# Up-projection of an MLP in fp32r with weight pieces stationary and 256 tokens moving, and the norm factor moved to the residual add

## The reference

```python
def rmsnorm(x, w):
    y = xf * lax.rsqrt(jnp.mean(xf * xf, axis=-1, keepdims=True) + EPS)
    return (y * w.astype(jnp.float32)).astype(x.dtype)

def sqrelu_mlp(h, w_up, w_down):        # w_up 2048 x 8192, w_down 8192 x 2048
    u = jax.nn.relu(h @ w_up)
    return (u * u) @ w_down

for layer in range(2):
    ...
    x = x + y.astype(x.dtype)           # y of the mixer or the attention
    h = rmsnorm(x, norm_mlp_w[layer])
    x = x + sqrelu_mlp(h, mlp_w_up[layer], mlp_w_down[layer]).astype(x.dtype)
return rmsnorm(x, final_norm_w)
```

## Time and profile before

| | |
|---|---|
| median of 3 runs | 2051.8 us (2050.81 to 2052.05) |
| span of the profiled execution, its own time | 2050.5 us |
| TensorE (PE) matmul busy | 2007.7 us, 98% |
| TensorE weight load (PEld) busy | 1655.0 us, 81% |
| DVE busy | 1422.5 us, 69% |
| ACT busy | 1019.8 us, 50% |
| DMA | 382.49 MB, mean 187 GB/s |

### The profile page before, as it was taken

How to read it: one execution, slowest core, us unless ns; L and a number is a source line. 1 busy time by engine, 2 the same in 40 slices (tenths; PEclk the granted TensorE clock), 3 DMA queues, 4 the chain that set the end, 5 groups by cost and what they waited for, 6 DMA issues and landing times.

```text
span 2050.5 us, 24784 instructions
## 1 busy us (share of the span) xinstructions
PE 2007.7 (98%) x9195; PEld 1655.0 (81%) x9195; DVE 1422.5 (69%) x1931; ACT 1019.8 (50%) x1343; POOL 43.3 (2%) x55
## 2 busy tenths in 40 slices
PE   8999999999999999999999999999999999999997
PEld 6888888877888788788887877878888888788886
DVE  5776678887467657756888677878548656855864
ACT  5566665454345435434555554555345434534543
POOL 1110110000000000000000000000000000000000
PEclk9999999999999999999999999999999999999999
DMA  8555546655656556556655544566566566556552
GB/s 291 171 171 204 184 156 211 189 175 196 199 178 205 189 190 192 189 192 191 198 174 197 165 140 149 186 193 196 185 192 197 185 191 196 183 192 196 185 192 100
DMA packets 191612, 382.49 MB, mean 187 GB/s; under 512 B 6184, under 2 KB 6448, under 8 KB 191408
## 3 DMA queue, kind: packets, MB, share of 16 engines
q1 hardware_dynamic: 190288, 377.58, 56.8%
q0 software_dynamic: 1216, 3.88, 0.6%
q10 hardware_dynamic: 32, 0.01, 0.0%
HBM read 379.34 MB, written 2.10 MB: 186 GB/s over the span
## 4 chain that ended last, share of the span: by engine, by line
PE 83%; DVE 9%; ACT 4%; issue 3%; DMA 0%; ACTq 0%; SPq 0%; DVEq 0%
PE acc L1018 27%; PE acc L1020 27%; PE acc L1019 27%; DVE turn L887 3%; DVE w_lo L701 3%; ACT w_hi L516 2%; PE bank L1029 1%; ACT stage L561 0%; PE bank L1108 0%; DVE b_lo L709 0%; DVE a_lo L713 0%; ACT L580 0%; PE bank L1118 0%; PE bank L1132 0%; ACT area L606 0%
## 5 line engine op out<-in xcount | busy, mean ns | idle before, releaser
L701 DVE TENSOR_TENSOR w_lo<-raw,w_hi 128x1024 fp32r<-128x1024 f32 x712 | 867.0, 1225 | 560.6 <-ACT w_hi L516 558.1
L516 ACT ACTIVATE w_hi<-raw 128x1024 fp32r<-128x1024 f32 x712 | 748.5, 1059 | 845.3 <-PE acc L1020 845.2
L1018 PE MATMUL acc<-w_hi,a_hi 128*128 128x512 f32 x1568 | 617.1, 394 | 5.0 <-DVE a_lo L713 4.7
L1020 PE MATMUL acc<-w_hi,a_lo 128*128 128x512 f32 x1568 | 611.9, 390 | 0.0
L1019 PE MATMUL acc<-w_lo,a_hi 128*128 128x512 f32 x1568 | 611.7, 390 | 0.0
L1018 PE MATMUL acc<-w_hi,b_hi 128*128 128x512 f32 x1280 | 500.2, 391 | 13.1 <-DVE b_lo L709 10.9
L1020 PE MATMUL acc<-w_hi,b_lo 128*128 128x512 f32 x1280 | 498.7, 390 | 0.0
L1019 PE MATMUL acc<-w_lo,b_hi 128*128 128x512 f32 x1280 | 498.7, 390 | 0.0
L1018 PEld LDWEIGHTS acc<-w_hi,a_hi 128*128 128x128 f32 x1568 | 295.0, 188 | 69.0 <-DVE a_lo L713 6.0
L1020 PEld LDWEIGHTS acc<-w_hi,a_lo 128*128 128x128 f32 x1568 | 294.8, 188 | 61.6
L1019 PEld LDWEIGHTS acc<-w_lo,a_hi 128*128 128x128 f32 x1568 | 295.0, 188 | 60.0
(11 more groups left out here) (152 smaller groups left out, 522.4 us busy)
## 6 DMA issues: line engine op xcount, KB each, us to landing
raw<-in_mlp_w_up SPq DMA_DIRECT2D x128, 1024.0 KB, 5.6
raw<-in_mlp_w_down SPq DMA_DIRECT2D x128, 1024.0 KB, 5.1
raw<-in_hyb_w_in SPq DMA_DIRECT2D x48, 1024.0 KB, 5.2
raw<-in_attn_w_qkv SPq DMA_DIRECT2D x20, 1024.0 KB, 5.1
raw<-in_hyb_w_out SPq DMA_DIRECT2D x16, 1024.0 KB, 5.2
raw<-in_attn_w_out SPq DMA_DIRECT2D x16, 1024.0 KB, 5.1
x<-in_x SPq DMA_DIRECT2D x4, 512.0 KB, 9.8
out_y<-x SPq DMA_DIRECT2D x4, 512.0 KB, 4.0
```

The source lines that it names most:

```text
L516: nc.scalar.activation(w_hi[:, h % RING], raw[:, h // 2, 2 * (h % 2):2 * (h % 2) + 2, :], ACT.Copy).then_inc(hi_ready, 1)
L701: nc.vector.tensor_tensor(w_lo[:, h % RING], raw[:, h // 2, 2 * (h % 2):2 * (h % 2) + 2, :], w_hi[:, h % RING].bitcast(F32), ALU.subtract) ...
L1018: nc.tensor.matmul(a, xh, wh, start=first, stop=False)
L1020: ins = nc.tensor.matmul(a, xl, wh, start=False, stop=last)
```

## The change

In an up block the operands change places: the stationary one is now a 128x128 piece of the weights, the moving one the 256 tokens of a row tile of `a_hi` or `a_lo`. The result comes out with hidden columns on the partitions and tokens along them, as the down blocks need it; the two halves of a bank hold two pieces of 128 hidden columns. The turn by DVE is gone for up blocks. A factor per token can't be applied per partition any more; since relu(s h) squared is s squared times relu(h) squared for positive s, the norm factor is squared (`rinv2`) and multiplied in where the down block's result is added to `x`.

```diff
-BY_QUADRANT = {"up", "res"}
+BY_QUADRANT = {"res"}
+AS_TURNED = {"up"}
...
+            def leave_up(slot):
+
+                b = slot.b - 1
+                act.wait_ge(turned_out, slot.count(N_TURNED, -1, INIT_HALVES))
+                for m in range(2):
+                    nc.scalar.activation(stage[:, m, :], acc[:, b % 2, m, :], ACT.Relu).then_inc(evac_act, 1)
+                for m in range(2):
+                    act.wait_ge(evac_act, slot.count(N_EVAC_ACT, -1, m + 1))
+                    nc.scalar.activation(stage[:, m, :], stage[:, m, :], ACT.Square).then_inc(squared, 1)
+
+            def up_hi(slot, j):
+
+                for m in range(2):
+                    act.wait_ge(squared, slot.count(N_SQUARED, -1, m + 1))
+                    nc.scalar.activation(b_hi[:, COLS * j + 2 * m:COLS * j + 2 * m + 2, :],
+                                         stage[:, m, :].rearrange("p (k s) -> p k s", k=2),
+                                         ACT.Copy).then_inc(turned_hi, 1)
...
+                if kind == "up" and k == 1:
+                    up_hi(slot, j)
...
+                ins = nc.vector.reciprocal(rinv[:, norm, :], rms[:, norm, :])
+                if norm in (1, 3):
+                    link(ins)
+                    ins = nc.vector.tensor_tensor(rinv2[:, norm, :], rinv[:, norm, :], rinv[:, norm, :], ALU.mult)
+                ins.then_inc(rinv_ready, 1)
...
+            def up_lo(slot, j):
+
+                for m in range(2):
+                    dve.wait_ge(turned_hi, slot.count(N_SPLIT, -1, INIT_HALVES + m + 1))
+                    to = slice(COLS * j + 2 * m, COLS * j + 2 * m + 2)
+                    nc.vector.tensor_tensor(b_lo[:, to, :], stage[:, m, :].rearrange("p (k s) -> p k s", k=2),
+                                            b_hi[:, to, :].bitcast(F32), ALU.subtract).then_inc(turned_out, 1)
...
+                        if norm is None:
+                            ins = nc.vector.tensor_tensor(xs, xs, y, ALU.add)
+                        else:
+                            ins = nc.vector.scalar_tensor_tensor(xs, y, rinv2[:, norm, tt:tt + 1], xs,
+                                                                 ALU.mult, ALU.add)
...
+                if kind == "up" and k == 2:
+                    up_lo(slot, j)
...
+                if BLOCKS[b][0] == "up":
+                    up_products(b, k).then_inc(half_used, 1)
+                    return
...
+            def up_products(b, k):
+
+                for e in range(2):
+                    kt = 2 * k + e
+                    xh, xl = a_hi[:, kt, :], a_lo[:, kt, :]
+                    for f in range(COLS):
+                        wh, wl = (w[:, k % RING, e, f * P:(f + 1) * P] for w in (w_hi, w_lo))
+                        a = acc[:, b % 2, f // 2, (f % 2) * SEQ:(f % 2 + 1) * SEQ]
+
+                        first, last = k == 0 and e == 0 and f % 2 == 0, k == HALVES - 1 and e == 1
+                        nc.tensor.matmul(a, wh, xh, start=first, stop=False, skip_group_check=True)
+                        nc.tensor.matmul(a, wh, xl, start=False, stop=False, skip_group_check=True)
+                        ins = nc.tensor.matmul(a, wl, xh, start=False, stop=last, skip_group_check=True)
+                return ins
```

More of the change, by code:

```diff
@@ L90 @@
 TURNED = {"xb", "gate", "q", "k", "g", "kv", "aq", "up", "res"}
-BY_QUADRANT = {"up", "res"}
+BY_QUADRANT = {"res"}
+AS_TURNED = {"up"}
 SPLIT = {"g", "up", "res"}
 PLAIN = TURNED - SPLIT
+THROUGH_TURN = TURNED - AS_TURNED
 FROM_STAGE = {"xb", "gate", "kv", "aq"}
 TURN_AT = {"aq": 0, "q": 3, "k": 3, "g": 4, "xb": 2, "gate": 2, "kv": 2}
-QUADRANTS_AT = {"up": {1: 4, 2: 6, 3: 6}, "res": {1: 4, 2: 6, 3: 6}}
+QUADRANTS_AT = {"res": {1: 4, 2: 6, 3: 6}}
 STATIONARY_STARTS = ({MIX_OUT0, MLP0, QKV0, ATT_OUT0, MLP1}
@@ L127 @@
 N_TURNED = total(TURNED, 2)
+N_TURNS = total(THROUGH_TURN, 2)
 N_SPLIT = total(SPLIT, 2)
@@ L229, in build @@
         rinv = sb("rinv", [P, 5, TT])
+        rinv2 = sb("rinv2", [P, 5, TT])
         soft = sb("soft", [P, 8, LRU_BLOCKS])
@@ L544, in leave @@
                 act.wait_ge(half_used, slot.halves(0))
+                if kind == "up":
+                    leave_up(slot)
+                    return
                 norm = NORM_OF[b]
@@ L560, in leave @@
                     else:
-                        ins = nc.scalar.activation(stage[:, tt, :], src, ACT.Relu if kind == "up" else ACT.Copy, scale=s)
+                        ins = nc.scalar.activation(stage[:, tt, :], src, ACT.Copy, scale=s)
                     ins.then_inc(evac_act, 1)
[L563 to L566, removed]
+            def leave_up(slot):
[12 more added lines that the diff above has]
+                                         ACT.Copy).then_inc(turned_hi, 1)
             def lru(n, step):
@@ L624, in post @@
                     square_sums(next_norm(b), j)
-                if kind in SPLIT and k == out_at(kind):
+                if kind == "up" and k == 1:
+                    up_hi(slot, j)
+                if kind in SPLIT - AS_TURNED and k == out_at(kind):
                     hi, _, kt, scale = target(b)
@@ L628, in post @@
                         turned_parts(hi, kt + 2 * m, None if scale is None else scale + 2 * m,
-                                     slot.count(N_TURNED, -1, INIT_HALVES + m + 1), m, kind in BY_QUADRANT)
+                                     slot.count(N_TURNS, -1, INIT_HALVES + m + 1), m, kind in BY_QUADRANT)
                 if k == 4 and kind == "res" and j == COLS - 1:
@@ L733, in inverse @@
                 dve.wait_ge(rms_ready, norm + 1)
-                nc.vector.reciprocal(rinv[:, norm, :], rms[:, norm, :]).then_inc(rinv_ready, 1)
+                ins = nc.vector.reciprocal(rinv[:, norm, :], rms[:, norm, :])
[3 more added lines that the diff above has]
+                ins.then_inc(rinv_ready, 1)
             def rotate():
@@ L876, in turn_quadrants @@
                     return
-                if k == min(at) and kind == "up":
-                    dve.wait_ge(squared, slot.count(N_SQUARED, 0))
-                if k == min(at) and kind == "res":
+                if k == min(at):
                     dve.wait_ge(evac_dve, slot.count(N_EVAC_DVE, 0))
-                src = stage if kind == "up" else x[:, :, j * NB:(j + 1) * NB]
+                src = x[:, :, j * NB:(j + 1) * NB]
                 src = src.rearrange("p t (k f c) -> p t k f c", k=COLS, f=QUADRANTS)
@@ L904, in post @@
                     dve.wait_ge(half_used, slot.halves(0))
+                    norm = NORM_OF[b]
+                    if norm is not None:
+                        dve.wait_ge(rinv_ready, norm + 1)
                     for tt in range(TT):
                         xs = x[:, tt, j * NB:(j + 1) * NB]
-                        nc.vector.tensor_tensor(xs, xs, acc[:, b % 2, tt, :], ALU.add).then_inc(evac_dve, 1)
+                        y = acc[:, b % 2, tt, :]
+                        if norm is None:
[3 more added lines that the diff above has]
+                                                                 ALU.mult, ALU.add)
+                        ins.then_inc(evac_dve, 1)
                 if k == 1:
@@ L928, in post @@
                     turn_quadrants(slot, k, kind, j)
-                if kind in TURNED and k == out_at(kind):
+                if kind == "up" and k == 2:
+                    up_lo(slot, j)
+                if kind in THROUGH_TURN and k == out_at(kind):
                     for m in range(2):
@@ L935, in post @@
                         elif kind in PLAIN:
-                            dve.wait_ge(turned, slot.count(N_TURNED, -1, INIT_HALVES + m + 1))
+                            dve.wait_ge(turned, slot.count(N_TURNS, -1, INIT_HALVES + m + 1))
                             nc.vector.tensor_copy(plain_target(kind, j)(m),
@@ L1037, in post @@
                 kind, j = BLOCKS[b]
-                if kind not in TURNED - BY_QUADRANT:
+                if kind not in THROUGH_TURN - BY_QUADRANT:
                     return
```

## The result

The changed kernel takes 2103.86 us (median of 4 runs, 2103.05 to 2104.97) against 2051.86 us before: the ratio is 1.0254, 95% interval 1.0242 to 1.0267. It is slower by 52.0 us. The forecast was slower, 2080.6 us, with a range from 2034 to 2116.

A forecast was written before the change was run, and what follows sets the result against it. The prediction took TensorE's matmul spacing, 226.7 ns a step, as the bound. Steps +41.0 us and waits -12.2 us gave +28.8 us on the 2050.5 us span; keeping the median's 1.3 us difference, 2080.6 us, range 2034 to 2116.

The forecast's parts named there:

- The sign: Whole kernel: slower, given 0.60; faster 0.35, within 0.2% 0.05; slower unless the step is below 115.3 ns.
- the forecast's own range: Whole kernel: up-block steps of 118 to 123 ns give 2068 to 2099 us; chance 0.46.
- The steps of 120.0 ns: Up blocks: 192 matmuls of 106.7 + 13.3 ns, 1.28 us more a block, +41.0 us over 32 blocks.
- The rival of 113.3 ns: Up blocks: extra belongs to the columns, blocks stay as long, only waits go: 2039.6 us; chance 0.28.
- that of 111: Up blocks: matmul with load runs as the float32 rows do, 111 ns a step: 2025 us; chance 0.06.
- that of 125 or more: Up blocks: load and stream hold each other up, steps of 125 to 136 ns: 2111 to 2179 us; chance 0.13.
- all three such waits: TensorE's waits for `a_lo` at the three stages after a residual stage: not touched by the change.
- The reason given for the step: Each fp32r matmul: loading the next weights takes 13.3 ns from the full-rate stream, once per matmul with its load.
- The waits: First down block of each group: eight waits of 1.53 us for `b_lo` go, -12.2 us.
- The residual add: Down blocks: scalar_tensor_tensor takes 680 to 952 ns, hidden by matmuls; tail 0 to +0.5 us, taken as 0.
- Issuing, "nothing is charged": TensorE: matmuls per microsecond double, but bursts go out some 28 and 109 ns apart, so no time is added.
- late weight cuts: TensorE: rival in which waits remain or move, for instance to weight cuts, +12 us on any case; given little chance.

The follow-up runs named there:

- written out: The changed kernel with TensorE's program written out for all 89 blocks instead of two loops over eight blocks: 2077.7 us.
- the epilogue alone: The changed kernel with the up blocks' products as before and all else as changed: 2038.9 us, ratio 0.9939 to the kernel before.
- the run with the short third product: The changed kernel with the third product of every up-block step made for the first 128 tokens alone: 2084.8 us in one run.
- These two runs: The kernel before with 64 stationary columns, in every second product of three (2073.7 us) or in nearly all matmuls (2072.6 us).

## Why the prediction was right, and what it missed

**The number.** The sign and the step are right, and 2103.9 us lie inside the range from 2034 to 2116. But they lie outside the forecast's own range, 2068 to 2099, whose step came true. That the wide range holds them is partly luck: its upper end was set for steps of 125 ns or more, which did not come, and not for what did add the time.

**The steps of 120.0 ns: right.** The forecast took 106.7 + 13.3 ns, and the trace has 120.0. The rival of 113.3 ns (an extra per column), that of 111 and that of 125 or more are out. In the sum the step was worth +41.0 us; the runs give 38.8 (written out against the epilogue alone). Of the difference 1.6 us are a side effect that the forecast missed: the up block at the head of each MLP now takes 1.28 us longer, so the last `a_lo` is less late. Its wait was 1.58 us before and is 0.78 now, twice; the forecast had all three such waits unchanged.

**The reason given for the step: not shown, and in one form wrong.** Two lengths fit an extra once per matmul with its load, and not one per column: 226.7 = 213.3 + 13.3 and 120.0 = 106.7 + 13.3. At half clock the extra is not there: the steps are 213 ns for 256 columns, as the 427 ns of the earlier trace rows are for 512. (There the granted clock reads 1.00, also for 13.30 to 16.20 us alone; after the gaps it reads 0.50.) But two lengths leave a rival that I did not test. In the changed kernel PEld is busy for 30.00 of 30.00 us, so its loads follow one another without a pause, and in the run with the short third product they do so 116 ns apart. A stream of 113.3 ns for 256 columns, held up by its loads to 120, would look the same. That the extra is time which the load takes from the stream was my reading. Loads of 64 columns end it in the form in which I held it, in proportion to the load: the steps grew to 230 ns. What the 13.3 ns are stays open. These two runs do not exclude a load that takes a fixed time.

**The waits: right.** -12.2 us expected, -12.9 measured with the epilogue alone. The low parts were to be 6.5 us early and are 7.1: they end at 497.2, and the seventh half comes 15.15 us after the first evacuation, as in the earlier trace rows (501.27 - 486.12), at 504.3.

**The residual add: right.** The price lay within its bounds of 680 to 952 ns, at 744 (the mean of 64 adds at L947), and is hidden: the epilogue alone loses nothing.

**Issuing, "nothing is charged": this step failed.** It was judged by bursts of 32 and 16 matmuls at one place, and these say only how fast ready instructions go out, not how they get there. The doubled number of matmuls makes the loop's body too long to be kept, and the steps in front of its jump are twice as fast, so that (this part is argued) they use up in half the time what was issued before the jump. Together that is 26.2 us, of which 17.6 are the four gaps and nearly all of the rest the half clock after them. I had looked for late weight cuts as the wait that could take the place of the old one, and not at TensorE's own program. The term is as large as half of the whole loss: -12.9 + 38.8 + 26.2 = 52.1 us, against 52.0 measured. (The three are differences along one chain of runs, so that they add up proves nothing; each is a measurement of its own part.) Without it the forecast would have been 3 us off (2080.6 against 2077.7 written out).

## What to carry to other kernels

Cost a matmul as its moving columns plus a fixed part, from the spacing of starts in the trace, not from durations: whoever halves the columns and doubles the matmuls pays the fixed part twice, here 13.3 ns each, and near 256 columns of fp32r against 128 stationary ones the loads are about to bind as well, or do already. Before adding instructions inside a loop, look at the instruction queue in the loop's window: if there are no packets, the body is kept, and growth can end that; if it has to be fetched, write the loop out or let it jump behind slow matmuls; here either gave the 26 us back. And when a change is made for its shorter epilogue, first try whether the old epilogue can merely be begun earlier and waited for in parts: here that gave 20 us, with not one matmul changed.

## What the runs showed of the hardware

- The time of an fp32r matmul's step beyond its columns at 2.4 GHz is the same for 512 and 256 moving columns, 13.3 ns (steps of 226.7 and 120.0), and absent at 1.2 GHz (213 ns for 256 columns where the granted clock was 0.50). With 64 stationary columns it is larger, 16.7 ns (230.0 - 213.3), and 16.5 in the mean where only every third load has 64.
- Loads of 128 columns in fp32r can follow one another at about 116 ns (the run with the short third product), although each is shown as lasting 188 to 194 ns.
- A backward jump on TensorE cost 4.0 to 4.6 us when the body (864 to 1152 matmuls) was fetched anew and the steps in front were of 120 ns, and nothing when they were of 227 ns (1152 matmuls, fetched anew as well). After such a gap the clock was granted at 0.50, for about 5.5 us at the first and 3 to 5 us at the other three of the changed kernel, and each step there took 213 ns.
- A body of 768 matmuls, each with its load, ran without one instruction packet between 600 and 950 us; one of 864 had 17.
